# A table of sums in DRAM that the expert outputs are added into by accumulating scatters, and the input rows loaded from two queues

## What is computed

```python
h = rmsnorm(x, norm_mix)
x = x + hybrid_mixer(h, ...)              # three branches, gated and merged
h = rmsnorm(x, norm_ffn)
x = x + hierarchical_moe(h, ...)          # this sum is what the change rewrites
out = rmsnorm(x, norm_final)

# inside hierarchical_moe: each token goes to 2 of 16 experts
for e in range(16):
    a = silu(t @ w_gate[e]) * (t @ w_up[e])
    out = out + gate[:, e:e+1] * (a @ w_down[e])
```

## Time and profile before

| | us |
|---|---|
| device time, median of 3 runs | 726.92 |
| lowest and highest | 726.73, 729.63 |
| device time of the profiled execution | 727.01 |
| its span | 725.2 |
| TensorE busy (matmuls) | 702.1 |
| VectorE, ScalarE, GpSimd busy | 518.5, 402.8, 148.4 |
| DMA traffic | 159.16 MB |

### The profile page before, as it was taken

How to read it: one execution, slowest core, us unless ns; L and a number is a source line. 1 busy time by engine, 2 the same in 40 slices (tenths; PEclk the granted TensorE clock), 3 DMA queues, 4 the chain that set the end, 5 groups by cost and what they waited for, 6 DMA issues and landing times.

```text
span 725.2 us, 10018 instructions
## 1 busy us (share of the span) xinstructions
PE 702.1 (97%) x3581; PEld 587.6 (81%) x3581; DVE 518.5 (72%) x536; ACT 402.8 (56%) x411; POOL 148.4 (20%) x151
## 2 busy tenths in 40 slices
PE   7999999999999999999999999999999999999990
PEld 6898888888888888888889868888888888888880
DVE  4688776898526062340735778999999999999984
ACT  6626665666523131221513537777777777777742
POOL 5320000000000000000000133433383338333123
PEclk9999999999999999999999999999999999999996
DMA  9685320000242333322583369999999999999486
GB/s 324 169 267 179 117 94 24 30 3 14 87 131 65 108 101 99 114 92 82 208 340 153 146 229 412 414 385 381 383 390 380 387 395 390 382 378 388 176 190 174
DMA packets 67298, 159.16 MB, mean 219 GB/s; under 512 B 6274, under 2 KB 37116, under 8 KB 63172
## 3 DMA queue, kind: packets, MB, share of 16 engines
q1 hardware_dynamic: 59520, 138.95, 52.6%
q0 software_dynamic: 7696, 19.80, 8.3%
q10 hardware_dynamic: 52, 0.01, 0.0%
HBM read 150.64 MB, written 15.73 MB: 229 GB/s over the span
## 4 chain that ended last, share of the span: by engine, by line
PE 86%; DMA 5%; DVE 4%; ACT 3%; issue 1%; POOL 1%; POOLq 0%; SPq 0%; DVEq 0%; ACTq 0%
PE ps L522 25%; PE ps L524 24%; PE ps L523 24%; DMA x<-y_rows 3%; PE ps L1662 2%; PE ps L1720 2%; PE ps L1612 1%; PE ps L1584 1%; DMA xn<-in_x 1%; PE ps L1442 1%; DMA y_rows<-ye,y_col 1%; PE ps L1688 1%; DVE soft L1984 1%; PE ps L1404 1%; ACT ring_hi L484 1%
## 5 line engine op out<-in xcount | busy, mean ns | idle before, releaser
L490 DVE TENSOR_TENSOR ring_lo<-raw_a,ring_hi 128x2048 fp32r<-128x2048 f32 (+2 forms) x58 | 115.5, 1995 | 97.0 <-ACT ring_hi L484 97.0
L490 DVE TENSOR_TENSOR ring_lo<-raw,ring_hi 128x2048 fp32r<-128x2048 f32 x71 | 162.2, 2291 | 9.2 <-ACT ring_hi L484 7.9
L484 ACT ACTIVATE ring_hi<-raw 128x2048 fp32r<-128x2048 f32 x71 | 136.3, 1920 | 20.2 <-PE ps L524 20.2
L484 ACT ACTIVATE ring_hi<-raw_a 128x2048 fp32r<-128x2048 f32 (+2 forms) x58 | 97.4, 1680 | 33.6 <-PE ps L524 30.6
L522 PE MATMUL ps<-hT_hi,ring_hi 128*128 128x512 f32 x288 | 113.4, 394 | 1.6 <-DVE hT_lo L1840 1.0
L524 PE MATMUL ps<-hT_hi,ring_lo 128*128 128x512 f32 x288 | 112.2, 390 | 0.0
L523 PE MATMUL ps<-hT_lo,ring_hi 128*128 128x512 f32 x288 | 112.2, 390 | 0.0
L522 PE MATMUL ps<-ring_hi,xT_hi 128*128 128x512 f32 x240 | 95.3, 397 | 0.1
L524 PE MATMUL ps<-ring_hi,xT_lo 128*128 128x512 f32 x240 | 94.0, 391 | 0.0
L523 PE MATMUL ps<-ring_lo,xT_hi 128*128 128x512 f32 x240 | 93.6, 390 | 0.0
L522 PEld LDWEIGHTS ps<-hT_hi,ring_hi 128*128 128x128 f32 x288 | 54.1, 188 | 13.0 <-issue 1.2
(11 more groups left out here) (372 smaller groups left out, 1272.8 us busy)
## 6 DMA issues: line engine op xcount, KB each, us to landing
raw<-in_w_down SPq DMA_DIRECT2D x25, 1024.0 KB
raw<-in_w_gate SPq DMA_DIRECT2D x47, 512.0 KB
raw<-in_w_up SPq DMA_DIRECT2D x47, 512.0 KB
raw_a<-in_w_in SPq DMA_DIRECT2D x15, 1024.0 KB
raw_a<-in_w_gate SPq DMA_DIRECT2D x17, 512.0 KB
raw_a<-in_w_up SPq DMA_DIRECT2D x17, 512.0 KB
raw_a<-in_w_down SPq DMA_DIRECT2D x7, 1024.0 KB
raw_a<-in_w_in SPq DMA_DIRECT2D x10, 512.0 KB, 8.1
```

Of the source, the lines that this page charges most:

```text
L484: act.activation(ring_hi[:, c[0] % SPLIT, 0:width], buf[:, 0:width], ACT.Copy).then_inc(hi_ready, 1)
L490: dve.tensor_tensor(ring_lo[:, s, 0:width], buf[:, 0:width], ring_hi[:, s, 0:width].bitcast(F32), ALU.subtract).then_inc(lo_ready, 1)
```

## The change

`y_rows` becomes `sum_rows`, a DRAM table with one row for each token. It is filled with `x2` (the residual after the mixer) instead of zeros: GpSimd stores blocks 0 to 2 right behind the store of the normed rows, and block 3 between two gathers. The scatters are the same 14, but add to the table (`compute_op=ALU.add`) and take their row numbers from `x_row`, the token's number. Since a scatter waits for the landing of the one before it, no two are in flight on one row. At the end four plain loads on SyncE's queue bring `x2` back, and the six loads, the two VectorE additions and the waits between them are gone. At the start, SyncE loads blocks 0 and 1 of `x` and ScalarE blocks 2 and 3; the four loads of gains move from ScalarE to SyncE, behind its two blocks.

```diff
-            for t in range(TB):
+            for t in (0, 1):
                 sp.dma_start(xn[:, t, :], x[0, t * P:(t + 1) * P, :]).then_inc(x_in[t], 16)
+            sp.dma_start(gain_rows[0:KD, :], norm_mix[0].rearrange("(k p) -> k p", p=P)).then_inc(gain_in, 16)
...
-            for t in range(PLAIN):
-                sp.dma_start(y_in[:, t, :], rows_of(t, 0)).then_inc(y_load[t], 16)
+            for t in range(TB):
+                sp.dma_start(x2[:, t, :], sum_rows[t * P:(t + 1) * P, :]).then_inc(y_back[t], 16)
...
-            for c in range(2 * TB):
-                pool.dma_start(y_rows[c * P:(c + 1) * P, :], zero_rows[:, :]).then_inc(y_zero, 16)
...
                 pool.dma_start(h2_rows[t * P:(t + 1) * P, :], h2[:, t, :]).then_inc(h2_out, 16)
+                if t < TB - 1:
+                    pool.dma_start(sum_rows[t * P:(t + 1) * P, :], x2[:, t, :]).then_inc(x2_out, 16)
...
-                pool.indirect_dma_start(y_rows[:, :], bass.IndirectOffsetOnAxis(y_col[b][:, :].bitcast(U32), 0),
-                                        ye[b][:, :], None, bounds_check=2 * S - 1, oob_is_err=False).then_inc(y_out[b], 16)
+                pool.indirect_dma_start(sum_rows[:, :], bass.IndirectOffsetOnAxis(y_col[b][:, :].bitcast(U32), 0),
+                                        ye[b][:, :], None, bounds_check=S - 1, oob_is_err=False,
+                                        compute_op=ALU.add).then_inc(y_out[b], 16)
...
             x_load(2, 0, None)
+            pool.dma_start(sum_rows[(TB - 1) * P:TB * P, :], x2[:, TB - 1, :]).then_inc(x2_out, 16)
             x_load(3, 1, 2)
...
-            pool.wait_ge(y_zero, 16 * 2 * TB)
+            pool.wait_ge(x2_out, 16 * TB)
...
-            for t in range(PLAIN):
-                pool.dma_start(x2[:, t, :], rows_of(t, 1), accum_op=ALU.add).then_inc(y_back[t], 16)
-            for t in range(PLAIN, TB):
-                pool.dma_start(x2[:, t, :], rows_of(t, 0), accum_op=ALU.add).then_inc(y_back[t], 16)
-            for t in range(PLAIN, TB):
-                pool.wait_ge(y_back[t], 16)
-                pool.sem_inc(pool_free, 1)
-                pool.dma_start(x2[:, t, :], rows_of(t, 1), accum_op=ALU.add).then_inc(y_back[t], 16)
...
-            act.dma_start(gain_rows[0:KD, :], norm_mix[0].rearrange("(k p) -> k p", p=P)).then_inc(gain_in, 16)
+            for t in (2, 3):
+                act.dma_start(xn[:, t, :], x[0, t * P:(t + 1) * P, :]).then_inc(x_in[t], 16)
...
-                if r == 0:
-                    act.wait_ge(y_zero, 16 * 2 * TB)
...
-                if t < PLAIN:
-                    dve.wait_ge(y_added, t + 1)
-                else:
-                    dve.wait_ge(y_back[t], 32)
+                dve.wait_ge(y_back[t], 16)
                 add_placed(t, t + 1)
```

More of the change, by code:

```diff
@@ L296, in build_trunk @@
     h2_rows = nc.dram_tensor("h2_rows", [S, D], F32, kind="Internal").ap()
-    y_rows = nc.dram_tensor("y_rows", [2 * S, D], F32, kind="Internal").ap()
+    sum_rows = nc.dram_tensor("sum_rows", [S, D], F32, kind="Internal").ap()
     ctx = ExitStack()
@@ L419, in build_trunk @@
         ye_free = sem("ye_free")
-        y_zero = sem("y_zero")
-        y_load = [sem(f"y_load{b}") for b in range(PLAIN)]
-        y_added = sem("y_added")
+        x2_out = sem("x2_out")
         wts_ready = sem("wts_ready")
@@ L540, in _ @@
             wkv = w_kv_mem[0]
-            for t in range(TB):
+            for t in (0, 1):
                 sp.dma_start(xn[:, t, :], x[0, t * P:(t + 1) * P, :]).then_inc(x_in[t], 16)
+            sp.dma_start(gain_rows[0:KD, :], norm_mix[0].rearrange("(k p) -> k p", p=P)).then_inc(gain_in, 16)
+            sp.dma_start(gain_rows[KD:2 * KD, :], norm_mem[0].rearrange("(k p) -> k p", p=P)).then_inc(gain_in, 16)
+            sp.dma_start(gain_rows[2 * KD:2 * KD + 2, :], pool_scale[0].rearrange("(k p) -> k p", p=P)).then_inc(gain_in, 16)
+            sp.dma_start(gain_rows[2 * KD + 2:3 * KD + 2, :], norm_ffn[0].rearrange("(k p) -> k p", p=P)).then_inc(gain_in, 16)
             sp.dma_start(raw_a[:, 0, 0:1024].rearrange("p (k n) -> p k n", k=4),
@@ L758, in _ @@
             pool.sem_inc(ye_free, 2)
-            step(pool.memset(zero_rows[:, :], 0.0))
             inverse_root(slice(TB, TB + MB), TB + MB)
@@ L800, in y_store @@
             def y_store(tile, b, earlier):
-                pool.tensor_copy(y_col[b][:, :], y_row[:, bass.ds(tile, 1)]).then_inc(y_col_set, 1)
+                pool.tensor_copy(y_col[b][:, :], x_row[:, bass.ds(tile, 1)]).then_inc(y_col_set, 1)
                 pool.wait_ge(y_col_set, tile + 1)
@@ L852, in _ @@
             y_store(NE - 3, 1, NE // 2 - 1)
-            for b in range(2):
-                pool.wait_ge(y_out[b], 16 * (NE // 2 - 1))
-                pool.sem_inc(pool_free, 1)
-            for t in range(PLAIN):
-                pool.dma_start(x2[:, t, :], rows_of(t, 1), accum_op=ALU.add).then_inc(y_back[t], 16)
-            for t in range(PLAIN, TB):
-                pool.dma_start(x2[:, t, :], rows_of(t, 0), accum_op=ALU.add).then_inc(y_back[t], 16)
-            for t in range(PLAIN, TB):
-                pool.wait_ge(y_back[t], 16)
-                pool.sem_inc(pool_free, 1)
-                pool.dma_start(x2[:, t, :], rows_of(t, 1), accum_op=ALU.add).then_inc(y_back[t], 16)
             pool.wait_ge(route_ready, 1)
```

16 lines of the change are left out of this document (removed).

## The result

| | before | changed |
|---|---|---|
| time, median | 728.15 us (726.73 to 729.65, 13 runs) | 731.09 us (729.32 to 733.24, 13 runs) |
| ratio, 95% interval | | 1.0041 (1.0029 to 1.0053): slower by 2.1 to 3.9 us |
| profiled execution / its span | 727.01 / 725.2 us | 732.18 / 730.4 us |
| first projection matmul of TensorE | 14.37 us | 17.01 us |
| start of its last matmul | 708.52 us | 719.65 us |

The page of the changed kernel: busy time, DMA share and GB/s in 40 slices, and the chain that ended last, by engine and by line.

What follows compares the result with a forecast made beforehand. TensorE, busy 97% of the span, was taken as the bound, with DMA able to fall behind in the middle. Span 725.2 + 1.2 + 7 - 5.3 = 728.1, plus 1.8 around it: 730 us against 726.92, range 722 to 738.

Steps and rivals of the forecast that it cites:

- Start: Loading of x: landings in order 0, 2, 1, 3 make the last square 1.15 us late; +1.2 us, range -1.4 to +2.5.
- the forecast's second case (packet by packet): Loading of x: engines alternate between queues, blocks 1 and 3 land together at 9.2, last square 2.5 us late.
- the gains now arrive behind block 1, before the transposes of block 1 can begin: Start: gains, moved behind SyncE's two x blocks, arrive in time for the transposes; no cost of their own.
- Stores of x2: Beside the first weights: the fourth store, 512 KB, takes 1.3 us from the weights' lead; the three early ones cost 0.
- Price of an accumulating scatter: Middle, each expert: an accumulated byte occupies an engine 2.1 times as long, so 2.6 us instead of 1.25, 1.3 more.
- Middle: Expert stage: 12 scatters and the stores cost 16.9 us against a lead of 11.1; with unevenness, +7 us.
- The 1.2 us for unevenness: Expert stage: 1.2 us added to the 5.8 us lateness because leads vary from chunk to chunk.
- End: After the last matmul: last addition begins behind TensorE at 709.1 instead of 714.97, less 0.6 given back; -5.3 us.
- give-back: End: GpSimd's inverse root of block 2 falls into VectorE's scaling, taking 1.47 us instead of 0.55; 0.6 us given back.
- rival 1: Middle: accumulation stays hidden if a scatter costs under 0.8 us more; 722.9 us, faster; chance 0.25.
- Rival 2: Middle: adding to DRAM slower than to SBUF, 2.7 us more a scatter, about 745; decides from 1.7 us; chance 0.12.
- rival 3: End: last scatter takes over 15 us from issue, so the table loads come behind TensorE; 734 us; chance 0.08.

Runs made afterwards that it cites:

- experiment 6: Before-kernel with changed start: 730.98 us; changed kernel with 16 warm-up multiplications, not 12: 729.97 us; changed kernel with gains on ScalarE ahead of its x blocks: 731.16 us.
- Experiments 2: Changed kernel with plain scatters in place of accumulating ones, part of the computation left out: 724.9 us, ratio 0.9958 to the kernel before.
- Experiment 3: Changed kernel with every second scatter plain, the others accumulating, part of the computation left out: 725.01 us, ratio 0.9952 to the kernel before.
- experiment 1: Changed kernel with all x blocks on SyncE and the gains on ScalarE, as in the kernel before: 728.33 us, ratio 0.9999 to the kernel before.

## Why the forecast held, and where its terms did not

730 us were forecast, 731.1 came, and the main mechanism is the one described: the accumulation takes DMA time, the lead runs out, TensorE waits, and the end gives back less than that. By terms:

- **Start**: forecast +1.2, measured +2.6 in the profiled execution. The landings came in the assumed order, but in pairs, 0 with 2 and 1 with 3. That is how the forecast's second case (packet by packet) has it, only that the second pair was there at 8.4 to 8.6 and not at 9.2. The 2.6 us add up as follows. The squares behind block 1: 1.15 us, as forecast. Block 1 at 8.42 instead of 7.88: 0.5. GpSimd's inverse root, which takes 1.47 us a block where a square takes 1.24, so that the last scaling is 2.0 us late and not 1.7: 0.3, a link that the forecast left out. The half clock: 0.6 (experiment 6), left out as well. There the step that failed is "the gains now arrive behind block 1, before the transposes of block 1 can begin ... no cost of their own". They arrive in front of these, but TensorE had been idle for 1.9 us by then, and the transposes behind ran at half clock. Nothing was gained by the second queue: the last block did land 0.6 us sooner, but the order of the blocks lost more than that.
- **Stores of x2**: forecast 1.3 us of lead; the lead at chunk 18 is 2.0 lower (7.5 instead of 9.5), if the stores are all of it.
- **Price of an accumulating scatter**: forecast 1.3 us more, measured 1.5; the rows' 422 / 197 gave a factor of 2.1; a row of the scatter takes 0.33 us where the plain one takes 0.16, which is the same factor, and the pace of the weights gives (1.25 + 1.5) / 1.25 = 2.2, if the plain one costs the assumed 1.25. The trace shows the lead gone at chunk 48, 559 us, not from 600 on: 7.5 us of lead, less 1.5 an expert, plus the 0.13 by which the DMA was quicker than TensorE. Experiments 2 and 3 leave no other cause.
- **Middle**: forecast +7, measured +6.75 (experiment 1). By the terms as measured: eleven experts at 1.5 us, 2.3 us of lead less at chunk 18, and 11.2 us of lead to use up (11.0 at chunk 84 before, -0.2 now) give 11 x 1.5 + 2.3 - 11.2 = 7.6 us at chunk 84, and 0.8 of it is made good behind. In the forecast's own sum, which goes to chunk 88, that chunk landed 16.0 us later than before (678.80 against 662.83), where 12 x 1.3 + 1.3 = 16.9 were forecast: the price was too low, but from chunk 84 to 88 the landings won 2.7 us back, as if the twelfth scatter did not count. That these two errors cancel is luck. The 1.2 us for unevenness, put in without a row, has its counterpart in the 1.4 us of lead that chunk 88 still had (split at 680.21) after TensorE had waited for chunks before it.
- **End**: forecast -5.3, measured -5.9. The last addition follows the last matmul at once. From the last matmul to the last two half additions it is 0.5 us in place of 6.45, the forecast 5.9 less. The give-back is there too, 0.8 us for the forecast's 0.6: GpSimd's inverse root takes 1.47 us, VectorE's scaling runs from 721.35 to 727.68 (6.3 us) where it took 5.5, and waits for GpSimd in between. But the output ends 2.7 us behind the scaling in place of 3.5, and that was not in the sum; why is not known. It happens to make up for the give-back.
- **The reference of the sum**: the two profiled executions differ by 5.2 us, the medians by 2.9. The middle of the changed one holds 8.5 = 6.8 + 1.7 us, and the 1.7 are the half clock near 401 us that the profiled execution of before happened not to have. Without it the difference of the traces is 3.5 us, inside the measured interval. The forecast for the difference, 730 - 726.92 = 3.1 us, fits that as well.

Of the rivals, 1 gave a threshold of 0.8 us for a scatter. Experiment 3 stands just below it with 0.74 and costs nothing, so the condition was right and the price was not met. Rival 2, 1.7 us and more, was missed by 0.2 us; rival 3 did not come, the loads of the table have 4.7 us of room or more. In rival 1 the result would have been 722.9; the kernels with the changed start in which the lead lasts have 724.9 (plain scatters), 725.0 (half of them accumulating) and 725.7 (spread slots), with a start that costs up to 1.4 us more than the 1.2 in that sum, and beside a kernel before whose median over more runs is 728.15 to 728.98 instead of 726.92.

## What to carry to other kernels

Before a DMA is made to do arithmetic, read the lead of the stream beside it: chunks landed against chunks used, at the begin and the end of the stage. A price per step is free up to (lead / steps), and what goes beyond it counts at every step; here it was a matter of 0.8 against 1.5 us. And where a gather or scatter fills only part of the partitions, spread the filled rows over all of them first: it cost two changed patterns here, was worth nothing while there was slack, and won back 5.9 us where taking out the addition won 6.0.

## What the runs showed of the hardware that was not expected

- The granted clock falls to half for 3 to 7 us near 400 us, in the routing stage, while the records show TensorE busy throughout. It cost about 1.7 us in six of the twelve traces (in the kernel before with the split start too), 3.2 us in two, and nothing in four. Executions of the kernel before differ by more, with spans from 724.8 us at a mean clock of 0.992 to 729.8 us at 0.985. The fall comes in or right behind a stretch of 32 matmuls of only 20 columns (396.28 to 400.22 us in the changed kernel, the fall at 399.5), but the traces without the fall have this stretch too. What brings it on was not settled; a difference of 2 us between two single traces says little until their granted clocks are laid beside each other.
- Four small multiplications more ahead of a gap go with a different clock behind it. With 12 of them the clock is at half for 3.4 or 6.8 us in all five traces with the start of the changed kernel, between 8.1 and 17.2 us, and TensorE is idle for 1.9 to 3.1 us in front of the gains; with 16 it stays at full in the one trace there is, with 1.3 us of idle time. The mean clocks of the other executions point the same way: 0.991 to 0.997 with 16, 0.985 to 0.992 in the changed kernel. Whether the work ahead of the gap or its length decides, no run separates.
- Accumulating into a DRAM table costs about as much per byte as accumulating into SBUF: 0.33 us a row against 0.16 is a factor of 2.1, as is 422 / 197 GB/s. GpSimd's own instruction for it takes 2.73 us on average where the plain one took 2.2.
- While the lead was still there (chunks 18 to 48), landings came every 19.6 us an expert, and every 19.0 behind it. Why they are faster when TensorE waits for them was not looked into.
